# Strassen's scheme for the z and gate projections of a branch in an eighteen-block decoder step

## What is computed

```python
h = rmsnorm(x, g_norm[l])
a_u, a_v, a_z, b_q, b_k, b_v, b_gd, b_z, c_q, c_z, gl = split_proj(h, w_in[l])
...
out_c = cross_attn(c_q, mk, mv) * jax.nn.silu(c_z)
x = x + merge(gl, b_gate[l], (out_a, out_b, out_c), w_branch[l], w_out[l])
...
gates = jax.nn.sigmoid(gate_logits + b_gate).reshape(*lead, N_BRANCH, D_MODEL)
proj = jnp.einsum('btic,icd->btid', br, w_branch)
return jnp.sum(gates * proj, axis=-2) @ w_out
```

## Time and profile before

| | us |
|---|---|
| median of 3 runs | 854.45 (854.24 to 855.84) |
| the profiled execution, first to last instruction (span) | 852.3 |
| TensorE busy | 842.5 |
| VectorE busy | 429.2 |
| ScalarE busy | 374.8 |
| CZ and GC with the attention between | 632.6 to 751.3 |

### The profile page before, as it was taken

One profiled execution on the slowest core, in us unless ns is written; L12 is line 12 of the kernel. 1 busy time (PEld: TensorE's weight loads), 2 busy tenths in 40 slices (PEclk: granted clock), 3 DMA queues, 4 the chain that ended last, 5 costly groups with the idle time before them and its releaser, 6 DMA issues.

```text
span 852.3 us, 16317 instructions
## 1 busy us (share of the span) xinstructions
PE 842.5 (99%) x6923; PEld 821.2 (96%) x6923; DVE 429.2 (50%) x742; ACT 374.8 (44%) x618; POOL 67.6 (8%) x122
## 2 busy tenths in 40 slices
PE   8999999999999999999999999999999999999997
PEld 8999999999999999999999999999889999999995
DVE  6527542735564376323336797554354544445534
ACT  7544446347666543422232353332234545533424
POOL 1001000000000222001012111001020000000000
PEclk9999999999999999999999999999999999999999
DMA  9324743331322759524366864216563432262302
GB/s 309 94 91 149 257 148 100 99 102 50 117 82 87 241 184 345 209 73 151 101 222 236 309 202 151 95 56 236 185 225 97 144 105 83 67 222 69 130 2 100
DMA packets 87204, 126.21 MB, mean 148 GB/s; under 512 B 3114, under 2 KB 73816, under 8 KB 87136
## 3 DMA queue, kind: packets, MB, share of 16 engines
q1 hardware_dynamic: 73328, 76.58, 27.6%
q0 software_dynamic: 13712, 48.57, 16.1%
q10 hardware_dynamic: 96, 0.06, 0.0%
HBM read 112.98 MB, written 12.22 MB: 147 GB/s over the span
## 4 chain that ended last, share of the span: by engine, by line
PE 98%; ACT 1%; DVE 1%; ACTq 0%; issue 0%; DVEq 0%
PE mm L1070 65%; PE mm L1027 5%; PE mm L1042 5%; PE mm L1016 3%; PE mm L1286 2%; PE mm L1368 2%; PE p L1001 1%; PE p L1003 1%; PE p L1002 1%; PE mm L1307 1%; PE mm L1306 1%; PE mm L1305 1%; PE p L1245 1%; PE p L1215 1%; PE p L1081 1%; PE p L1184 1%
## 5 line engine op out<-in xcount | busy, mean ns | idle before, releaser
L1070 PE MATMUL mm<-h_lo,w_hi 128*128 128x260 f32 (+1 forms) x1088 | 222.1, 285 | 0.0
L1070 PE MATMUL mm<-h_hi,w_hi 128*128 128x260 f32 (+1 forms) x1088 | 219.0, 283 | 0.0
L1070 PE MATMUL mm<-h_hi,w_lo 128*128 128x260 f32 (+1 forms) x1088 | 218.6, 282 | 0.0
L1497 DVE TENSOR_TENSOR w_lo<-raw,w_hi 128x1024 fp32r<-128x1024 f32 x130 | 158.2, 1220 | 83.8 <-ACT w_hi L543 82.7
L1070 PEld LDWEIGHTS mm<-h_lo,w_hi 128*128 128x128 f32 x1088 | 167.7, 188 | 3.6 <-issue 3.3
L1070 PEld LDWEIGHTS mm<-h_hi,w_hi 128*128 128x128 f32 x1088 | 167.6, 188 | 0.0
L1070 PEld LDWEIGHTS mm<-h_hi,w_lo 128*128 128x128 f32 x1088 | 167.5, 188 | 0.0
L543 ACT ACTIVATE w_hi<-raw 128x1024 fp32r<-128x1024 f32 x130 | 135.7, 1052 | 10.6 <-DMA raw<-in_w_mem_kv_dram 6.3
L1070 PE MATMUL mm<-x_lo,w_hi 128*128 128x260 f32 (+1 forms) x448 | 96.2, 284 | 0.0
L1070 PE MATMUL mm<-x_hi,w_hi 128*128 128x260 f32 (+1 forms) x448 | 95.3, 283 | 0.0
L1070 PE MATMUL mm<-x_hi,w_lo 128*128 128x260 f32 (+1 forms) x448 | 95.1, 282 | 0.0
(11 more groups left out here) (388 smaller groups left out, 1339.2 us busy)
## 6 DMA issues: line engine op xcount, KB each, us to landing
raw<-in_w_in_dram SPq DMA_DIRECT2D x43, 1024.0 KB, 5.3
raw<-in_w_branch_dram SPq DMA_DIRECT2D x12, 1024.0 KB, 5.0
raw<-in_w_mem_kv_dram SPq DMA_DIRECT2D x8, 1024.0 KB, 5.8
gate<-in_cache_mem_k_dram POOLq DMA_DIRECT2D x16, 512.0 KB, 6.2
tok<-in_cache_mem_v_dram POOLq DMA_DIRECT2D x14, 512.0 KB, 5.0
tok<-in_state_gla_dram POOLq DMA_DIRECT2D x8, 512.0 KB, 7.5
out_dram<-tok POOLq DMA_DIRECT2D x8, 512.0 KB, 7.2
work<-scr_q POOLq DMA_DIRECT2D x8, 512.0 KB, 4.8
```

The costliest lines, as they stand in the source:

```text
L1070: ins = MM(mm[:, j % 2, a, 0:c1 - c0], wp[:, j, k, :], xp[:, k, c0:c1], start=(k == 0 and wp is w_hi and xp is xl), stop=(k == KT - 1 and ...
L1497: V.tensor_tensor(w_lo[:, j], raw[:, j // 2, :, (j % 2) * P:(j % 2 + 1) * P], f32(w_hi[:, j]), ALU.subtract).then_inc(split_done, 1)
```

## The change

CZ and GC are worked in 8 pairs of output tiles. The 256 x 1024 block of weights of a pair is taken as a 2 x 2 matrix: contraction tiles 0 to 3 and 4 to 7 (A11, A12 for the first output tile, A21, A22 for the second), and h as a 2 x 2 matrix of contraction halves and token halves. In place of the 8 products of quarters there are 7 (P1 to P7, the Winograd form of Strassen's scheme), each of 4 contraction tiles x 3 parts = 12 matmuls of 260 columns. For it:

- sums and differences of the quarters of h (T1 to T4) are made once, by VectorE in the hooks of block PA (t_parts, t_lo) and ScalarE (t_hi), into the place of gate, of h itself and of the buffers state and rows;
- sums of the weights (S1 to S4) are made by VectorE for each pair, in place in raw and in work (pair_sums, last_sum), and seven half-size units for each pair are split, in a ring of eight slots of w_hi and w_lo; a unit's slot is free when the product that read its predecessor is done (wait_slot);
- the results are combined in PSUM and around it: ScalarE copies P1 from one bank to the next so that P6 adds onto it (pair_copy), keeps a copy of the sum after P6 (pair_keep) and of P5 (pair_five), VectorE adds two quarters (add_low, add_high), ScalarE evacuates the four quarters one by one;
- P4 and P3 of a pair stand behind P1 of the next pair. The attention's hooks keep their order: a pair has two, one ahead of P6 and one behind P2;
- the gate of GC goes to t1 and no longer to gate, and the load of x for the end, now into gate, waits for the end of GC (L517 before). Several semaphores are merged, and the product of the sample tokens' c_z with the attention moves from the hook of the last CZ tile to one two tiles later.

The core of the diff:

```diff
+FAST = ("CZ", "GC")
+BEFORE = NAMES[BLK[FAST[0]] - 1]
+PAIRS = 4 * len(FAST)
+FIRST_TILE = KT * BLK[FAST[0]]
+UNIT = {"A11": 0, "S2": 1, "S3": 2, "S1": 3, "A12": 4, "S4": 5, "A22": 6}
+ORDER = [("P1", 0), ("P5", 0), ("P2", 0), ("P6", 0), ("P1", 1), ("P7", 0), ("P4", 0), ("P6", 1), ("P5", 1), ("P7", 1), ("P2", 1)]
+for _q in range(2, PAIRS):
+    ORDER += [("P1", _q), ("P4", _q - 1), ("P6", _q), ("P5", _q), ("P7", _q), ("P2", _q)]
+ORDER.append(("P4", PAIRS - 1))
...
+        t_home = {"T2": (t2_hi[:, :, :], t2_lo[:, :, :]), "T4": (quarter(h_hi, 0, 1), quarter(h_lo, 0, 1)),
+                  "T1": (t1_hi[:, :, :], t1_lo[:, :, :]), "T3": (t3_hi[:, :, :], t3_lo[:, :, :])}
+        t_sum = {"T1": quarter(t1, 0, 0), "T3": quarter(t1, 0, 1), "T2": quarter(t1, 1, 1), "T4": quarter(t1, 1, 0)}
+        T_ORDER = ("T2", "T4", "T1", "T3")
+        moving = {"P1": (quarter(h_hi, 0, 0), quarter(h_lo, 0, 0)), "P2": (quarter(h_hi, 1, 0), quarter(h_lo, 1, 0)),
+                  "P3": (quarter(h_hi, 1, 1), quarter(h_lo, 1, 1)), "P4": t_home["T4"], "P5": t_home["T1"],
+                  "P6": t_home["T2"], "P7": t_home["T3"]}
+        weight = {"P1": "A11", "P2": "A12", "P3": "S4", "P4": "A22", "P5": "S1", "P6": "S2", "P7": "S3"}
...
+        def slot(unit, q):
+
+            return (7 * q + UNIT[unit]) % 8
...
+        def banks(q):
+
+            return bank(4 * PAIRS - q), bank(4 * PAIRS + 1 - q), bank(4 * PAIRS + 2 - q)
...
+        def wait_slot(eng, unit, q):
+
+            m = 7 * q + UNIT[unit] - 8
+            if m < 0:
+                eng.wait_ge(prod_done, FIRST_TILE - 3 + (m + 8) // 2)
+            else:
+                held = next(u for u in UNIT if UNIT[u] == m % 7)
+                wait_product(eng, next(n for n in weight if weight[n] == held), m // 7)
...
+            def pair_copy(q):
+
+                wait_product(act, "P1", q)
+                act.wait_ge(evac_done, FIRST_TILE - 1 + 2 * q)
+                A(banks(q)[1], banks(q)[0], ACT.Copy).then_inc(sem("pair_copied"), 1)
+
+            def pair_keep(q):
+
+                wait_product(act, "P6", q)
+                if q == 0:
+                    act.wait_ge(stage_used, ST["PA"] + KT)
+                else:
+                    act.wait_ge(sem("pair_added"), 2 * q)
+                A(u2_copy, banks(q)[1], ACT.Copy).then_inc(sem("pair_copied"), 1)
+
+            def pair_five(q):
+
+                wait_product(act, "P5", q)
+                A(p5_copy, banks(q)[2], ACT.Copy).then_inc(sem("pair_copied"), 1)
...
+            def pairs(q):
+
+                name, p = FAST[q // 4], q % 4
+                if q == 0:
+                    pair_copy(0)
+                    t_hi(3)
+                    att_hi(0)
+                    last_hi(0)
+                    pair_leave_first(0)
+                    pair_ahead(1, 0)
+                else:
+                    if q >= 2:
+                        pair_copy(q)
+                    pair_leave_low(q - 1)
+                    last_hi(q)
+                    pair_leave_last(q - 1)
+                    pair_ahead(q + 1, 0)
+                pair_keep(q)
+                hooks(name, 2 * p)
+                if q == 0:
+                    pair_copy(1)
+                pair_five(q)
+                pair_ahead(q + 1, 1)
+                pair_ahead(q + 1, 2)
+                if q > 0:
+                    pair_leave_first(q)
+                hooks(name, 2 * p + 1)
+                if q == PAIRS - 1:
+                    pair_leave_low(q)
+                    pair_leave_last(q)
 
             def att_hi(h):
 
...
+                wh, wl = unit_of(w_hi_units, unit, q), unit_of(w_lo_units, unit, q)
+                xh, xl = moving[name]
+                for k in range(KH):
+                    for wp, xp in ((wh, xl), (wl, xh), (wh, xh)):
+                        last = MM(out, wp[:, k, :], xp[:, k, :], start=(first_mm and k == 0 and xp is xl), stop=(k == KH - 1 and wp is wh and xp is xh),
+                                  skip_group_check=True)
...
+                else:
+                    product("P1", q)
+                    product("P4", q - 1)
+                    product("P3", q - 1)
+                    hooks(name, 2 * p)
+                    product("P6", q)
+                    product("P5", q)
+                    product("P7", q)
+                    product("P2", q)
+                    hooks(name, 2 * p + 1)
...
+            def pair_sums(q):
+
+                dve.wait_ge(sem("unit_lo"), 4 * q + 1)
+                link(V.tensor_tensor(raw_part(q, "S3"), raw_part(q, "A11"), raw_part(q, "A21"), ALU.add))
+                V.tensor_tensor(raw_part(q, "S1"), raw_part(q, "A21"), raw_part(q, "A22"), ALU.add)
+                V.tensor_tensor(s2_sum, raw_part(q, "S3"), raw_part(q, "A22"), ALU.add).then_inc(sem("sums"), 1)
+
+            def last_sum(q):
+
+                dve.wait_ge(sem("unit_lo"), 4 * q + 4)
+                V.tensor_tensor(raw_part(q, "S4"), s2_sum, raw_part(q, "A12"), ALU.add).then_inc(sem("sums"), 1)
+
...
+            def add_low(q):
+
+                wait_product(dve, "P7", q)
+                dve.wait_ge(sem("pair_copied"), copied("P5", q))
+                if q >= 1:
+                    dve.wait_ge(evac_done, FIRST_TILE + 2 * q)
+                V.tensor_tensor(c22, banks(q)[1], p5_copy, ALU.add).then_inc(sem("pair_added"), 1)
+
+            def add_high(q):
+
+                wait_product(dve, "P3", q)
+                dve.wait_ge(sem("pair_copied"), copied("P6", q))
+                V.tensor_tensor(c12, banks(q)[2], u2_copy, ALU.add).then_inc(sem("pair_added"), 1)
...
+            def pairs(q):
+
+                name, p = FAST[q // 4], q % 4
+                if q == 0:
+                    t_lo(3)
+                    att_lo(0)
+                if q > 0:
+                    add_high(q - 1)
+                last_lo(q)
+                pair_ahead(q + 1, 0)
+                hooks(name, 2 * p)
+                pair_ahead(q + 1, 1)
+                add_low(q)
+                pair_ahead(q + 1, 2)
+                hooks(name, 2 * p + 1)
+                if q == PAIRS - 1:
+                    add_high(q)
...
             pool.wait_ge(sem("oc_lo"), CH + 1)
+            pool.wait_ge(prod_done, first("GC") + KT)
```

More of the change, by code:

```diff
@@ new lines, in last_hi @@
+            def last_hi(q):
+                act.wait_ge(sem("sums"), 4 + 2 * q + 2)
+                wait_slot(act, "S4", q)
+                wait_slot(act, "A22", q)
+                if slot("S4", q) < 7:
+                    ins = A(both(w_hi_units, "S4", q), raw_both(q, 1), ACT.Copy)
+                else:
+                    A(unit_of(w_hi_units, "S4", q), raw_part(q, "S4"), ACT.Copy)
+                    ins = A(unit_of(w_hi_units, "A22", q), raw_part(q, "A22"), ACT.Copy)
+                ins.then_inc(hi_ready, 2)
@@ L947, in _ @@
                     act.wait_ge(sem("mix_hi"), AH)
-                if name == "GC":
-                    act.wait_ge(stage_used, ST["PA"] + KT)
+                if name in FAST:
+                    for p in range(4):
+                        pairs(4 * FAST.index(name) + p)
+                    continue
                 def body(it, g):
@@ new lines, in pair_ahead @@
+            def pair_ahead(q, part):
+                if q == PAIRS:
+                    if part == 0:
+                        lo(FIRST_TILE + 2 * PAIRS, 0)
+                    elif part == 2:
+                        lo(FIRST_TILE + 2 * PAIRS + 1, 1)
+                elif part == 0:
+                    unit_lo("A11", q)
+                    pair_sums(q)
+                elif part == 1:
+                    unit_lo("S2", q)
+                else:
+                    sums_lo(q)
+                    unit_lo("A12", q)
+                    last_sum(q)
```

306 lines of the change are left out of this document (258 added, 48 removed).

## The result

| | before | changed |
|---|---|---|
| median of the runs, us | 855.29 (6 runs, 854.24 to 856.33) | 858.25 (6 runs, 857.63 to 859.14) |
| profiled execution, us | 854.45 | 858.03 |
| its span, us | 852.3 | 856.1 |

The ratio is 1.0032, 95% interval 1.0020 to 1.0043: the changed kernel is about 0.3% slower. A second set of runs gave 1.0039 (1.0025 to 1.0053). The forecast was 854.8 with a range of 850.5 to 859.0. The range holds the time; the likeliest case, no change, does not.

A forecast was written before the change was run, and what follows sets the result against it. TensorE bound the kernel before; after the change VectorE's and ScalarE's in-order queues close each head's loop. Start -1.6, two loops -0.6 and tail +2.5 give +0.3 us on 854.45: 854.8 us, range 850.5 to 859.0.

The forecast's parts named there:

- the likeliest case, no change: Whole kernel: time within 0.2% (1.7 us) of the kernel before, given 45%.
- The walk: Queue times followed from one head's scores to the next: VectorE and ScalarE close the loop at 29.2 us, against 29.5 before.
- a sign of being wrong: Waits at other products, such as P7 behind the kept copy or P4 behind the C22 addition, would show the forecast wrong.
- Rival A: Both blocks: helper work stays covered, TensorE stays bound and all 11.5 us are gained, 843.0 us; 5%.
- The unknown copy from PSUM to PSUM: ScalarE's copy, absent from the earlier trace: nearest 0.38 us, with 2.9 us of cover, costing nothing at 0.3 or 0.8.
- steps (6) and (7): VectorE's unbroken stretch from S4/A22 low part to next head's v low, then hand-over to TensorE: 13.12 us.
- Rival B: Loop pieces as short as their low bounds: loop about 28.2 us, TensorE waits 1.0 less in each, 851.4 us; 20%.
- tail: From head 3's scores to the stage's end, TensorE's again: 26.2 us against 23.7, 2.5 lost.
- rival D: TensorE's idling drops its clock to 1.2 GHz: two products behind each of eight waits cost 23 us, 878; 2%.
- the sentence on the sample product: Moving the sample product later, like renaming semaphores, was said to cost nothing, with no wait getting longer.
- rival C: Hand-overs around exponentials and in VectorE's stretch cost 0.05 us more each: 1.2 a loop, 4 in all, 858.8; 28%.
- The edits costed at nothing: T sums and splits in PA (13.6 us uncovered), weight transfers, the load of x, renamed semaphores: all hidden or nothing.

The follow-up runs named there:

- e2_nosums: The changed kernel without VectorE's four sums of weight quarters per pair (one replaced by a one-element copy; results not valid): 852.75 us, ratio 0.9961.
- e6_soft: The changed kernel with exp table loaded before the kept copy, row maxima before the quarter sums, last low parts after normalisation, in even pairs: 854.71 us, ratio 0.9990.
- e7_both: The changed kernel with e6_soft's order plus, in odd pairs, the next head's q, k, v splits and the head's product moved earlier: 849.59 us, ratio 0.9937.
- e10_both_pt: e7_both with the turned probabilities' low part ahead of VectorE's last sum of quarters, except in the sample product's pair: 848.81 us, ratio 0.9926.

## Why the prediction was right or wrong

**The bound, the loop and the waits: right.** Theory and kernel agree in the places (L1242 for v low, L1457 for the normalisation) and in the sizes: 1.5 forecast and 1.44 measured ahead of the first scores, 2.4 and 2.24 ahead of the first transposes, 1.6 and 1.58 to 1.62 ahead of the later scores, 1.0 and 0.78 ahead of the later transposes. (The walk counts from the last matmul's place, the trace 0.16 later; in the walk's terms the four are 1.60, 2.40, 1.74 to 1.78 and 0.94.) VectorE's sums count 0.60 and 0.73, where 0.60 and 0.71 were taken. Its load is 23.7 of a loop where 25 was forecast, ScalarE's 20.3 to 20.9 where the sum had 22. One wait came at a product that the forecast had named as a sign of being wrong: 0.43 us at P4 behind the C22 addition, in the third loop alone. Rival A fell on this queue, as e2_nosums shows. The unknown copy from PSUM to PSUM takes 0.37 to 0.40, as taken, and VectorE's stretch from the S4/A22 low part to the next scores is 13.17 (685.52 to 698.69) against 13.12 of steps (6) and (7). Rival B is out with it: the pieces are not short.

**Where the 3.2 us between 854.8 and 858.03 are.** The walk put PC's first product at 751.7 and it came at 755.1. By its terms:

| term | forecast | measured |
|---|---|---|
| scores of head 0 | 639.3 | 639.5 |
| head 0 to 1 | 27.8 | 29.7 (28.2 where the clock held) |
| head 1 to 2 | 29.2 | 29.5 |
| head 2 to 3 | 29.2 | 30.2 |
| tail | 26.2 | 26.3 |

**The step that failed is in rival D:** "so waits of 1 to 2.4 us should leave it at 2.4 GHz", at 2%. It was drawn from one stretch in which TensorE was busy half of 2 us and kept its clock. That stretch was no sure ground itself: in e6_soft TensorE was busy 1.08 of the same 2 us, and its clock fell a microsecond behind them. The longest of the eight waits was enough, in one profiled execution and not in another; the price was 1.5 us and not 23, since one wait in eight was followed by it. With the clock held the same kernel took 856.63.

**The second is the sentence on the sample product:** "nothing, no wait gets longer". Loop 2 to 3 is 0.7 us longer than loop 1 to 2, forecast as equal. In it two rows of VectorE and then ScalarE's read:

```profile
711.93 1.22 DVE L2121 TENSOR_TENSOR pT_lo<-p,pT_hi 128x1024 fp32r<-128x1024 f32 x1 [0.21 <-ACT pT_hi L1110]
713.07 0.22 DVE L2132 TENSOR_TENSOR t<-t,qsT 128x64 f32<-128x64 f32 x1
...
710.50 0.48 ACT L1015 ACTIVATE t<-mm,prm 128x260 f32<-128x260 f32 x1
710.88 1.02 ACT L1110 ACTIVATE pT_hi<-p 128x1024 fp32r<-128x1024 f32 x1
713.32 0.26 ACT L855 ACTIVATE x_hi<-t 128x64 fp32r<-128x64 f32 x1 [1.42 <-DVE t L2132]
713.48 0.37 ACT L994 ACTIVATE mm<-mm 128x260 f32<-128x260 f32 x1
713.78 0.46 ACT L1015 ACTIVATE t<-mm,prm 128x260 f32<-128x260 f32 x1
714.14 0.50 ACT L1015 ACTIVATE t<-stage,prm 128x260 f32<-128x260 f32 x1
714.54 1.05 ACT L976 ACTIVATE w_hi<-raw 128x1024 fp32r<-128x1024 f32 x1
```

The sample product (64 elements, 0.22 us) stands on VectorE behind the turned probabilities; ScalarE waits 1.42 us for it, and only then copies P1, empties two quarters (0.46 and 0.50 with the sigmoid's bias, 0.39 without it in CZ) and splits S4 and A22. The walk has that split at P3's end plus 0.20 (713.61 + 0.20 = 713.8 by the start of the values' products); it begins at 714.54, 0.7 later. This is read from the trace; no run moved the sample product alone.

**The third is rival C, at a small size.** From scores to transposes a head takes 9.65 and not 9.59, from P3's end to VectorE's low parts 1.44 (684.08 to 685.52) and not 1.28, and VectorE's stretch 13.17 and not 13.12: with the products between, 0.3 us a loop where C had put 1.2. The edits costed at nothing show no wait of their own: the T sums in PA, the weight transfers and the load of x leave the waits outside the two blocks about as they were, 1.3 us the longest, as in the earlier trace rows.

So the time came out beyond 0.2% by a sum of three: 1.5 us of clock, 0.7 of the sample segment, 1.2 left over in the start, three segments and the tail, which I put down to hand-overs, all of one sign; 0.2 came back, since 1.9 us lay around the span in place of 2.1. The mechanism that ate the gain was the forecast one. That the range holds the time is in part luck: its upper end was set by hand-overs of 4 us, which were 1.2, and the clock, which the range left out, and the samples' product, taken as nothing, made up the rest. What the forecast did not ask is whether the loop of 29.2 us is the scheme's or only its order's: by e7_both and e10_both_pt it is the order's.

## What to carry to other kernels

When a change takes work from the bounding engine and gives it to two helpers, do not stop at their busy shares: walk the in-order queues from one step of the bounding engine to its next, and price the loop. Then ask of every operation in that loop whether anything waits for it before the next one in the queue is wanted; moving those behind, in all the places at once, gave back 9 us here, where one move alone lost 5, nearly all of it by a fallen clock behind the longer waits. And where a forecast ends within a few tenths of a per cent of zero, look at the signs of the small terms left out: hand-overs, a fallen clock and a side product all made it slower here, and the forecast's middle had none of them.
